# In-projection of a hybrid decoder step: how the recurrent states leave the core

## The chip, the cores and the metric

The kernel runs on one core of one Trainium2 chip. The metric is the device time of one execution in microseconds (us). The engines are TensorE (PE: matmuls, its weight loads are PEld), VectorE (DVE), ScalarE (ACT), GpSimd (POOL) and SyncE (SP). SP and ACT also issue most of the DMAs, each into a queue of its own, and both queues are served by the same 16 DMA engines. An engine executes its instructions in the order in which they are written, and waits on semaphores (wait_ge).

## The reference

One inference step of a hybrid layer for a prompt of 2048 tokens (with 16 meta tokens ahead of it, 2064 rows) and for 8 sample rows with a paged cache. The part that matters here is the recurrent branch and what it returns:

```python
def rg_lru_branch(xr, gr, conv_buf, h0, lp):
    xc, conv_new = causal_dwconv(xr, conv_buf, lp['rnn_conv_w'], lp['rnn_conv_b'])
    ...                                   # gates r and i from 8 blocks of 64x64, a = exp(log_a)
    u = jnp.sqrt(-jnp.expm1(2.0 * log_a)) * (i * xc.astype(jnp.float32))
    h = linear_recurrence(a, u, h0.astype(jnp.float32))
    y = h * jax.nn.gelu(gr.astype(jnp.float32))
    return y.astype(xr.dtype), h[:, -1], conv_new
```

h[:, -1] is 512 numbers for the prompt (output rnn_h_prompt) and 8 x 512 for the samples (rnn_h_sample). Everything is fp32.

## The kernel before

All activations are kept transposed: channels on the 128 partitions, the 2080 token columns (2064 prompt, 8 sample, 8 of padding) along the row, in 5 blocks of 416. The in-projection is a list of 21 chunks of 128 output channels. A chunk is 5 blocks, and a block is 24 matmuls of 128x416 (8 pieces of the inner dimension, each as three products of split fp32 halves, L2154). PE writes block j of a chunk into PSUM bank j, DVE copies it to ZS (L1603), ACT stores it to DRAM.

Chunks 0 to 8 give the inputs of the recurrent branch (xrT, grT in DRAM) and the forget logits. Chunks 9 to 20 are four groups c = 0 to 3 of three chunks (q, k, v of 128 channels), written as a hardware loop of two turns with two groups each (`with e.Fori(0, 2) as i` and `for u in range(2)`, c = 2i + u). Beside these matmuls each group also runs 128 channels of the recurrent branch, in this order:

- ACT waits until the group before has its result mixT stored (r_st, L1157), and loads RX from xrT (L1158). RX is both the input and, later, the result.
- DVE makes the causal convolution RC out of RX (L1680, three times L1683, and three small ones for the samples, the last is L1695). It does so in turn with the copies of the q chunk's five blocks: copy 0, step, copy 1, step, and so on.
- PE, after the first block of the k chunk, waits for all copies of q and turns the tail of q (L2218), then waits for the convolution and does the gate matmuls (L2225, L2226). After each of the other blocks of k there is another pair of gate matmuls.
- ACT makes the gates, the decay RA and the factor RW, DVE multiplies, scans (L1728 writes the states h over all columns into RW) and adds the samples' step (L1732, semaphore r_sc). Then DVE writes mixT's values into RX (L1737, r_y).
- ACT, in its handling of the v chunk: after block 2 it stores the states (L1207, L1209), after block 3 it stores RX to mixT (L1213).

The rows of k and v are outputs with tokens as rows. So PE turns each block with four transposes into PSUM bank 5 (turn_rows, L2211), ACT copies the bank to a buffer TS (take_rows, L1134 and L1135) and stores it as rows of 512 bytes (L1138, L1142). There are 11 such events a group; t_pe counts PE's side, t_ev ACT's copies, and the two slots of TS are released by t_st[0] and t_st[1], which count landed DMAs. PE turns block j-1 of a chunk after it has computed block j, and block 4 of v right after the turn of block 3, at the group's end (L2237).

The state stores of the kernel before take the last prompt column of RW, [128 partitions x 1], and the 8 sample columns, [128 x 8], and write each element to its place in DRAM, where the 128 channels lie side by side and the samples 2048 bytes apart: 128 + 1024 elements of 4 bytes a group. The semaphore r_ho counts them; ACT waits for it before it overwrites RW in the next group, and at the end of the phase.

After the loop, SP loads the first head's q and k (fetch_head(0), L545 to L550; it waits for the last matmul, the q and k stores and POOL's memsets), ACT waits for all stores and counts up phase_end, and the attention phase begins when these loads have landed (L1747, L1226) and all engines have counted phase_end.

Of the kernel before, what the change touches and what calls it, by code (L numbers as in the profile page):

```python
# [17 lines left out]
ACT = mybir.ActivationFunctionType  # L18
AX = mybir.AxisListType

P = 128
# [14 lines left out]
TPR = NMETA + SEQ  # L36
NS = 8
TP = 2080
# [168 lines left out]
def build(nc, a, out):  # L207
    ctx = ExitStack()
    with ctx:
# [3 lines left out]
        def sem(name):  # L213
            return ctx.enter_context(nc.semaphore(name))
# [19 lines left out]
        identF = sb("identF", [P, P], F32)  # L234
# [31 lines left out]
        TS = sb("TS", [P, 2, 4, P], F32, m1)  # L266
        RX = sb("RX", [P, TP + 3], F32, m1)
        RC = sb("RC", [P, TP], F32, m1)
        RW = sb("RW", [P, TP], F32, m1)
# [134 lines left out]
        t_pe = sem("t_pe")  # L404
# [9 lines left out]
        r_gw = sem("r_gw")  # L414
        r_gl = sem("r_gl")
        r_st = sem("r_st")
        r_ho = sem("r_ho")
        r_conv = sem("r_conv")
        r_gate = sem("r_gate")
        r_act = sem("r_act")  # L420
# [92 lines left out]
        @block.sync  # L513
        def _(e):

            for s in (*x_st, *t_st, *z_st, r_st, r_gate, r_act, r_ho, r_y, t_pe, t_ev, pv, kf, df, vd, mr, *ao_st, od_s,
                      at_s, *tt_st, tt_ev, *go_st, gcv, tt_pe, y_tp, y_tk):
                e.sem_inc(s, 1)

# [517 lines left out]
        def _(e):  # L1037
# [92 lines left out]
            def take_rows(ev, slot, stored, j, kv, c):  # L1130
# [12 lines left out]
                if j == NB - 1:  # L1143
                    e.dma_start(one_k[kv][:, f], TS[NMETA:NMETA + NS, slot, 3]).then_inc(t_st[slot], 16)

            with e.Fori(0, 2) as i:

                plan = []
                count = [0, 0]
                for v in range(22):  # L1150
                    m = v % 11
                    plan.append((v % 2, count[v % 2]))
                    count[v % 2] += 16 * (1 if m == 0 else 3 if m in (5, 10) else 2)
                for u in range(2):
                    c = 2 * i + u
                    n = 9 + 3 * c
                    e.wait_ge(r_st, 16 * c + 1)  # L1157
                    e.dma_start(RX[:, 3:3 + TP], xrT[bass.ds(c * P, P), :]).then_inc(r_ld, 16)  # L1158
                    e.wait_ge(r_gate, 5 * c + 1)
                    e.wait_ge(c_gw, 1)  # L1160
                    for g, w in enumerate((a["w_rg_a"], a["w_rg_x"])):
                        for b in range(2):
                            e.dma_start(gw[64 * b:64 * b + 64, g, 64 * b:64 * b + 64], w[0][2 * c + b])\
                                .then_inc(r_gw, 16)

                    def event(m):
                        slot, before = plan[11 * u + m]
                        return 4 + 22 * i + 11 * u + m, slot, (128 if slot == 0 else 0) + count[slot] * i + before

                    for j in range(NB):  # L1170
                        store_block(n, j, qT[bass.ds(c * P, P), :], z_st)
                    take_tail(*event(0))
                    slot = event(0)[1]
                    e.dma_start(qrow[:, bass.ds(c * P, P)], TS[NMETA:NMETA + NS, slot, 0]).then_inc(t_st[slot], 16)
                    for j in range(NB):
                        store_block(n + 1, j, kT[bass.ds(c * P, P), :], z_st)

                        e.wait_ge(r_gate, 5 * c + j + 2)
                        if j:
                            e.wait_ge(r_u, 5 * c + j)  # L1180
                        e.sem_inc(go, 1)
                        e.activation(RT[:, 0], PS[:, 7, 0:BW], ACT.Tanh, bias=hb[:, bass.ds(c, 1), 1], scale=0.5)\
                            .then_inc(r_act, 1)
                        e.activation(RT[:, 1], PS[:, 6, 0:BW], ACT.Tanh, bias=hb[:, bass.ds(c, 1), 0], scale=0.5)\
                            .then_inc(r_act, 1)
                        e.wait_ge(r_act, 22 * c + 4 * j + 3)
                        if j == 0:
                            e.wait_ge(r_ho, 32 * c + 1)
                            e.wait_ge(r_y, c + 1)
                        e.sem_inc(go, 1)  # L1190
                        e.activation(RW[:, cols(j)], RT[:, 1], ACT.Tanh, bias=sp[:, bass.ds(c, 1), 0],
                                     scale=sp[:, bass.ds(c, 1), 0]).then_inc(r_act, 1)
                        e.activation(RA[:, cols(j)], RT[:, 1], ACT.Exp, bias=sp[:, bass.ds(c, 1), 6],
                                     scale=sp[:, bass.ds(c, 1), 6]).then_inc(r_act, 1)
                        take_rows(*event(1 + j), j, 0, c)
                    e.wait_ge(r_u, 5 * c + 5)
                    e.dma_start(RC[:], grT[bass.ds(c * P, P), :]).then_inc(r_gl, 16)
                    e.wait_ge(r_act, 22 * c + 21)
                    e.activation(RW[:], RW[:], ACT.Sqrt, scale=0.25).then_inc(r_act, 1)
                    for j in range(NB):  # L1200
                        take_rows(*event(6 + j), j, 1, c)
                        if j == 1:
                            e.wait_ge(r_gl, 16 * c + 16)
                            e.activation(RC[:], RC[:], ACT.Gelu_apprx_tanh).then_inc(r_act, 1)
                        if j == 2:
                            e.wait_ge(r_sc, c + 1)
                            e.dma_start(out["rnn_h_prompt"][0].rearrange("o n -> n o")[bass.ds(c * P, P), :],  # L1207
                                        RW[:, TPR - 1:TPR]).then_inc(r_ho, 16)
                            e.dma_start(out["rnn_h_sample"][0].rearrange("s n -> n s")[bass.ds(c * P, P), :],  # L1209
                                        RW[:, TPR:TPR + NS], allow_slow_non_contiguous=True).then_inc(r_ho, 16)  # L1210
                        if j == 3:
                            e.wait_ge(r_y, c + 2)
                            e.dma_start(mixT[bass.ds(DATT + c * P, P), :], RX[:, 3:3 + TP]).then_inc(r_st, 16)  # L1213

            e.wait_ge(t_st[0], 865)
            e.wait_ge(t_st[1], 737)
            e.wait_ge(r_st, 65)
            e.wait_ge(r_ho, 129)
            for s in z_st:
                e.wait_ge(s, 257)  # L1220
            e.wait_ge(r_act, 22 * 4 + 1)
            e.wait_ge(t_ev, 49)
            e.sem_inc(phase_end, 1)
            e.wait_ge(c_att2, 2)
            e.wait_ge(st_ld, 80)
# [304 lines left out]
        def _(e):  # L1530
# [125 lines left out]
            with e.Fori(0, 2) as i:  # L1656
                g_steps.start(i, 2 * 13)
                for u in range(2):
                    c = 2 * i + u
                    n = 9 + 3 * c  # L1660
                    ev = 4 + 11 * c
                    one = bass.ds(c, 1)

                    def tap(k):
# [459 lines left out]
        def _(e):  # L2124
# [75 lines left out]
            with e.Fori(0, 2) as i:  # L2200
                for u in range(2):
                    c = 2 * i + u
                    n = 9 + 3 * c
                    ev = 4 + 11 * c

                    def turn_rows(done, ev, j):

                        e.wait_ge(g_ev, done)
                        e.wait_ge(t_ev, ev + 1)
                        for m, (o, w) in enumerate(seg(j)):  # L2210
                            mm = e.transpose(PS[0:w, 5, m * P:(m + 1) * P], ZS[:, j, o:o + w], identF[:])  # L2211
                        mm.then_inc(t_pe, 1)

                    def after_k(j):
                        if j == 0:
                            e.wait_ge(g_ev, 5 * n + 10)
                            e.wait_ge(t_ev, ev + 1)
                            e.transpose(PS[0:TAIL, 5, 0:P], ZS[:, NB - 1, 3 * P:BW], identF[:]).then_inc(t_pe, 1)  # L2218
                        else:
                            turn_rows(5 * (n + 1) + j - 1 + 6, ev + j, j - 1)  # L2220

                        e.wait_ge(r_conv, c + 1)
                        e.wait_ge(r_gw, 64 * c + 64)
                        e.wait_ge(r_act, 22 * c + (4 * j - 1 if j else 1))
                        e.matmul(PS[:, 6, 0:BW], gw[:, 0], RC[:, cols(j)], start=True, stop=True)  # L2225
                        e.matmul(PS[:, 7, 0:BW], gw[:, 1], RC[:, cols(j)], start=True, stop=True).then_inc(r_gate, 1)  # L2226

                    def after_v(j):
                        if j == 0:
                            turn_rows(5 * (n + 1) + 4 + 6, ev + 5, NB - 1)  # L2230
                        else:
                            turn_rows(5 * (n + 2) + j - 1 + 6, ev + 5 + j, j - 1)

                    chunk(n, (1 + u) % 2)
                    chunk(n + 1, u % 2, after_k)
                    chunk(n + 2, (1 + u) % 2, after_v)
                    turn_rows(5 * (n + 2) + 4 + 6, ev + 10, NB - 1)  # L2237
            e.wait_ge(g_mm, 5 * NIN)
            e.wait_ge(t_pe, 49)
            e.wait_ge(r_gate, 21)  # L2240
            e.sem_inc(phase_end, 1)

# [372 lines left out]
```

## Time and profile before

| | |
|---|---|
| device time, 3 runs | 3356.98, 3363.10, 3363.46 us, median 3363.1 |
| the profiled execution | 3355.78 us, its span 3353.6 us |
| TensorE busy | 91% of the span |
| granted TensorE clock | 0.942 of full speed, mean |
| the four groups of the in-projection | about 335 to 694 us of the span |
| first matmul of the attention phase | 724.96 us |

The profile's times are counted from the start of the span. A query of the trace can be cut to a window of it. The granted clock is given as a share of full speed; 1.00 is the 2.4 GHz level, 0.50 the 1.2 GHz level.

### The profile page before, as it was taken

Reading aid. Unit: us, or ns where it says so; the run is one execution under the profiler, and the core shown is the slowest. Engines: PE = TensorE matmul, PEld = TensorE weight load, DVE = VectorE, ACT = ScalarE, POOL = GpSimd, SP = SyncE. Lnnn points to the kernel's source line nnn. Section 1 sums busy time; section 2 is a strip of 40 time slices with the busy share of each in tenths; the row PEclk is TensorE's granted clock in tenths of the full one; section 3 lists DMA queues with packets and bytes.
Section 4 is the critical chain, followed back from the end, with each engine's and each line's share of the span. In section 5 each row is a group of like instructions: output and inputs, shape, how many; then the busy total and the mean of one; then the engine's idle time right before and its main releaser. Section 6 shows DMA issues by size and latency. Waiting matters only on the chain.

```text
span 3353.6 us, 46822 instructions
## 1 busy us (share of the span) xinstructions
PE 3037.8 (91%) x15400; PEld 2659.0 (79%) x15400; DVE 1447.2 (43%) x1910; ACT 757.9 (23%) x1529; POOL 1212.9 (36%) x575
## 2 busy tenths in 40 slices
PE   4798998957788888897899999999999998999998
PEld 4798987843354545455898999999999998999998
DVE  4212433348566555534415445555445554222221
ACT  5100332212232333333202000000000002434343
POOL 1011111133566565633766222222222222455443
PEclk7899999967799898998899999999999999999999
DMA  5211343355787677754345111111111114555553
GB/s 182 94 65 55 90 104 94 86 106 160 237 250 231 182 228 236 229 174 136 113 132 154 44 47 51 51 42 48 45 42 51 51 38 155 183 182 188 180 194 110
DMA packets 253580, 422.52 MB, mean 126 GB/s; under 512 B 49265, under 2 KB 156954, under 8 KB 248906
## 3 DMA queue, kind: packets, MB, share of 16 engines
q1 hardware_dynamic: 167986, 322.58, 30.8%
q10 hardware_dynamic: 85152, 97.07, 9.6%
q8 instruction: 68, 1.11, 0.1%
q0 software_dynamic: 288, 1.05, 0.1%
q14 instruction: 86, 0.70, 0.1%
HBM read 337.21 MB, written 83.46 MB: 125 GB/s over the span
## 4 chain that ended last, share of the span: by engine, by line
PE 69%; DMA 7%; POOL 7%; DVE 6%; issue 5%; SPq 4%; ACT 2%; ACTq 0%; POOLq 0%; DVEq 0%
PE PS L2452 33%; PE PS L2154 13%; PE PS L2534 4%; PE PS L2536 4%; PE PS L2535 4%; POOL prod L905 3%; DMA Kpg<-in_cache_k 2%; PE PS L2346 2%; SPq L581 2%; PE PS L2443 1%; SPq L574 1%; DMA xin<-in_x_prompt 1%; PE PS L2135 1%; DVE YT L2097 1%; DMA mixT<-RX 1%
## 5 line engine op out<-in xcount | busy, mean ns | idle before, releaser
L2452 PE MATMUL PS<-MH,VS 128*128 128x416 f32 x4000 | 1086.9, 352 | 11.2 <-POOL VS L968 9.0
L2452 PEld LDWEIGHTS PS<-MH,VS 128*128 128x128 f32 x4000 | 750.1, 188 | 23.2 <-issue 12.3
L2452 PE MATMUL PS<-ML,VS 128*128 128x416 f32 x2000 | 701.4, 351 | 0.0
L962 POOL TENSOR_TENSOR VR<-VR,gains 128x1024 f32<-128x1024 f32 x52 | 98.7, 1898 | 791.6 <-PE PS L2452 694.9
L2452 PEld LDWEIGHTS PS<-ML,VS 128*128 128x128 f32 x2000 | 376.7, 188 | 4.2 <-issue 0.8
L1025 POOL TENSOR_TENSOR DL<-DR,DH 128x1408 fp32r<-128x1408 f32 x80 | 258.6, 3233 | 286.1 <-ACT DH L1446 286.0
L905 POOL TENSOR_TENSOR prod<-Kpg,qb 128x1024 f32<-128x1024 f32 x118 | 284.0, 2407 | 174.0 <-DMA Kpg<-in_cache_k 137.9
L2346 PE MATMUL PS<-PT,VA 128*65 128x416 f32 (+16 forms) x816 | 340.0, 501 | 4.0 <-ACT PT L1307 3.5
L2534 PE MATMUL PS<-GH,DH 128*128 128x416 f32 x880 | 314.3, 357 | 16.2 <-DVE GL L2079 8.6
L2154 PE MATMUL PS<-XH,WH 128*128 128x416 f32 x840 | 307.2, 366 | 19.8 <-issue 11.6
L2536 PE MATMUL PS<-GH,DL 128*128 128x416 f32 x880 | 310.5, 353 | 0.0
L2535 PE MATMUL PS<-GL,DH 128*128 128x416 f32 x880 | 308.4, 350 | 0.0
L2255 PE MATMUL PS<-KA,QA 68*128 68x512 f32 (+3 forms) x360 | 222.1, 639 | 90.1 <-DVE MP L1757 55.8
L1307 ACT ACTIVATE PT<-PS 128x416 f32<-128x416 f32 (+16 forms) x408 | 186.5, 459 | 501.1 <-PE PS L2332 335.6
L2154 PE MATMUL PS<-XH,WL 128*128 128x416 f32 x840 | 297.1, 354 | 0.0
L2154 PE MATMUL PS<-XL,WH 128*128 128x416 f32 x840 | 296.5, 353 | 0.0
L1419 ACT ACTIVATE GC<-GC 128x416 f32<-128x416 f32 x110 | 60.8, 553 | 824.6 <-DVE GC L2032 746.1
L1757 DVE TENSOR_REDUCE MP<-PS 128x1 f32<-128x512 f32 (+3 forms) x360 | 206.2, 600 | 83.6 <-PE PS L2255 49.8
L2062 DVE TENSOR_TENSOR GP<-PS,R 128x416 f32<-128x416 f32 x110 | 64.9, 592 | 364.9 <-PE PS L2452 364.6
L2255 PEld LDWEIGHTS PS<-KA,QA 68*128 68x128 f32 (+1 forms) x360 | 73.8, 206 | 179.6 <-DVE MP L1757 105.0
L1806 DVE TENSOR_REDUCE scw<-prod 128x16 f32<-128x1024 f32 x128 | 155.4, 1214 | 102.2 <-POOL prod L905 101.5
L841 POOL CAST WH<-WR 128x1024 fp32r<-128x1024 f32 x21 | 24.3, 1158 | 461.1 <-PE PS L2154 454.2
(273 smaller groups left out, 4501.7 us busy)
## 6 DMA issues: line engine op xcount, KB each, us to landing
Kpg<-in_cache_k SPq DMA_DIRECT2D x256, 256.0 KB, 4.2
Vpg<-in_cache_v SPq DMA_DIRECT2D x256, 256.0 KB, 4.1
DR<-in_w_down SPq DMA_DIRECT2D x80, 704.0 KB, 4.1
gT<-GO ACTq DMA_DIRECT2D x110, 208.0 KB, 1.9
VR<-in_w_up SPq DMA_DIRECT2D x44, 512.0 KB, 3.5
GRb<-gT SPq DMA_DIRECT2D x31, 416.0 KB, 5.1
WR<-in_w_stream SPq DMA_DIRECT2D x21, 512.0 KB, 3.6
GRa<-gT SPq DMA_DIRECT2D x24, 416.0 KB, 5.8
```

What stands on the lines that cost most here:

```text
L905: e.tensor_tensor(prod[:, g % 4], Kpg[:, g % 4], qb[:, v].unsqueeze(1).to_broadcast([P, 2, DATT]), ALU.mult).then_inc(kpp, 1)
L1025: e.tensor_tensor(DL[h][:], DR[:, h], DH[h][:].bitcast(F32), ALU.subtract).then_inc(d_lo, 1)
L1307: e.activation(PT[0:kr, t % 3, 0:n], PS[0:kr, (u + t) % 2, 0:n], ACT.Exp, scale=0.125).then_inc(ex, 1)
L1757: e.tensor_reduce(MP[0:rows, qt, pc:pc + 1], PS[0:rows, banks[p % len(banks)], 0:n], AX.X, ALU.max).then_inc(mx, 1)
L1806: e.tensor_reduce(sc[:, v, 2 * g:2 * g + 2, :], p.rearrange("p b (h d) -> p b h d", d=HD), AX.X, ALU.add)\
L2154: mm = e.matmul(PS[:, j, 0:BW], w[:, u, k], x[:, k, cols(j)], start=(k == 0 and q == 0), stop=(k == KC - 1 and q == 2))
L2255: mm = e.matmul(o[:, 0:n], QA[0:HD + 4, v, qt * P:qt * P + rows], KA[0:HD + 4, v, k0:k0 + n], start=True, stop=not diag)
L2346: e.matmul(PS[0:HD + 1, 4 + (u + j) % 2, o:o + n], VA[0:kr, u, kt], PT[0:kr, t % 3, 0:n], start=(kt == 0), stop=t in ENDS).then_inc(pv, 1)
L2452: mm = e.matmul(PS[:, j, 0:BW], w[:, u, k], x[:, k, cols(j)], start=(k == 0 and q == 0), stop=(k == KC - 1 and q == 2))
L2534: e.matmul(PS[:, v, 0:BW], DH[h][:, k], GH[:, r, m], start=(kk == 0), stop=False)
L2535: e.matmul(PS[:, v, 0:BW], DH[h][:, k], GL[:, r, m], start=False, stop=False)
L2536: e.matmul(PS[:, v, 0:BW], DL[h][:, k], GH[:, r, m], start=False, stop=(kk == FC - 1))\
```

## The change

The last prompt state and the sample states are now the columns TPR-1 to TP-1 of RW, 17 in all (8 of them padding). PE turns them with one transpose into 17 rows of 128 in PSUM bank 5, as a twelfth event of the group; ACT copies them to a slot of TS and stores row 0 to rnn_h_prompt and rows 1 to 8 to rnn_h_sample, each row 512 bytes. The element stores and the semaphore r_ho go. The counts of events per group go from 11 to 12.

```diff
+            def take_states(ev, slot, stored, c):
+                e.wait_ge(t_pe, ev + 2)
+                e.wait_ge(t_st[slot], stored + 1)
+                e.activation(TS[0:TP - TPR + 1, slot, 0], PS[0:TP - TPR + 1, 5, 0:P], ACT.Copy).then_inc(t_ev, 1)
+                e.wait_ge(t_ev, ev + 2)
+                f = bass.ds(c * P, P)
+                e.dma_start(out["rnn_h_prompt"][0][:, f], TS[0:1, slot, 0]).then_inc(t_st[slot], 16)
+                e.dma_start(out["rnn_h_sample"][0][:, f], TS[1:1 + NS, slot, 0]).then_inc(t_st[slot], 16)
...
                         if j == 0:
-                            e.wait_ge(r_ho, 32 * c + 1)
                             e.wait_ge(r_y, c + 1)
...
-                        if j == 2:
-                            e.wait_ge(r_sc, c + 1)
-                            e.dma_start(out["rnn_h_prompt"][0].rearrange("o n -> n o")[bass.ds(c * P, P), :],
-                                        RW[:, TPR - 1:TPR]).then_inc(r_ho, 16)
-                            e.dma_start(out["rnn_h_sample"][0].rearrange("s n -> n s")[bass.ds(c * P, P), :],
-                                        RW[:, TPR:TPR + NS], allow_slow_non_contiguous=True).then_inc(r_ho, 16)
                         if j == 3:
                             e.wait_ge(r_y, c + 2)
                             e.dma_start(mixT[bass.ds(DATT + c * P, P), :], RX[:, 3:3 + TP]).then_inc(r_st, 16)
+                    take_states(*event(11), c)
...
                     turn_rows(5 * (n + 2) + 4 + 6, ev + 10, NB - 1)
+                    e.wait_ge(r_sc, c + 1)
+                    e.wait_ge(t_ev, ev + 12)
+                    e.sem_inc(go, 1)
+                    e.transpose(PS[0:TP - TPR + 1, 5, 0:P], RW[:, TPR - 1:TP], identF[:]).then_inc(t_pe, 1)
```

PE's wait on t_ev means: ACT has copied the eleventh event (the last block of v) out of bank 5. In DVE's program only the count changes (ev = 4 + 12c): its waits on t_pe for the q chunk's blocks now name one event later than before, all of them issued by PE ahead of the block that DVE copies.

## Rows read from the trace of the kernel before

**Rows 1.** Waits of PE, 335 to 700 us: us in total, times, longest.

```profile
PE PS L2218 <- DVE ZS L1603: 13.0, 2, 7.3
PE PS L2154 <- issue: 11.6, 1, 11.6
...
PE PS L2225 <- DVE RC L1695: 1.8, 2, 0.9
```

**Rows 2.** The chain of waits, 396 to 530 us: start, us, what.

```profile
417.30 14.45 DMA mixT<-RX
...
431.91 5.54 DMA RX<-xrT
...
452.53 1.75 PE PS L2225 x2
454.28 1.39 PE PS L2226 x2
455.66 5.51 PE PS L2154 x24
...
461.62 0.70 PE PS L2225 x2
...
463.01 4.54 PE PS L2154 x24
```

**Rows 3.** DMA issues: queue, count, KB each, median us from issue to landing.

```profile
xT<-xst ACTq DMA_DIRECT2D x16, 512.0 KB, 3.8
...
RX<-xrT ACTq DMA_DIRECT2D x4, 1040.0 KB, 5.1
...
mixT<-RX ACTq DMA_DIRECT2D x4, 1040.0 KB, 14.2
```

**Rows 4.** Tile RW, the sample states' store: ns min/median/max, first and last start.

```profile
L1209 ACTq DMA_DIRECT2D out_rnn_h_sample<-RW x4: 394/396/403, 412.7 to 690.4; - x4
```

**Rows 5.** Timeline of ACT, 504.6 to 505.2 us: the same store in the second group.

```profile
504.81 0.40 ACTq L1209 DMA_DIRECT2D out_rnn_h_sample<-RW  x1
```

**Rows 6.** Stretches: length, busy PE, PEld, DVE, ACT, POOL; clock, DMA share, GB/s.

```profile
462.00:482.00 20.00, 20.00 (x100) 17.29 (x99) 5.06 (x9) 9.70 (x20) 1.44 (x2) 1.00 0.20 65
508.00:512.90 4.90, 0.66 (x4) 0.37 (x4) 0.00 (x0) 0.21 (x2) 2.57 (x2) 0.94 0.83 51
...
417.30:428.60 11.30, 11.30 (x62) 11.17 (x61) 0.59 (x1) 0.64 (x2) 1.31 (x1) 1.00 1.10 48
428.60:431.70 3.10, 3.10 (x18) 3.06 (x17) 0.00 (x0) 0.00 (x0) 0.00 (x0) 1.00 0.87 293
...
694.60:706.70 12.10, 0.00 (x0) 0.00 (x0) 0.00 (x0) 0.64 (x2) 3.02 (x1) 0.58 1.11 48
706.70:720.70 14.00, 0.00 (x0) 0.00 (x0) 0.00 (x0) 0.00 (x0) 0.00 (x0) 0.50 0.87 215
```

**Rows 7.** The chain of waits, 618 to 650 us.

```profile
641.68 4.74 PE PS L2154 x24
```

**Rows 8.** Lines L2200 and L2407, PE's loops: their branches, ns min/median/max.

```profile
L2200 PEldq COMPARE_BRANCH  x2: 79/5979/11879, 508.4 to 693.6; - x2
...
L2407 PEldq COMPARE_BRANCH  x3: 76/223/4338, 1102.0 to 1471.0; - x3
```

**Rows 9.** The chain, 690 to 770 us, and from the waits of SP.

```profile
700.07 20.61 DMA Kst<-kT
...
SPq L625 <- ACTq L1223: 17.7, 1, 17.7
```

**Rows 10.** Timeline 413 to 422.5 us: last turn of a group, ACT's copy of it.

```profile
416.09 0.66 PE L2211 MATMUL PS<-identF,ZS 128*128 128x128 f32 x4 [0.73 <-ACT TS L1135]
...
418.22 0.25 ACT L1135 ACTIVATE TS<-PS 32x128 f32<-32x128 f32 x1
```

**Rows 11.** A stretch in which PE idles, columns as in rows 6.

```profile
2821.90:2824.70 2.80, 0.00 (x0) 0.00 (x0) 2.80 (x2) 1.77 (x2) 1.89 (x1) 1.00 0.78 299
```

**Rows 12.** Line L1142, ACT's issues of the v rows: ns min/median/max.

```profile
L1142 ACTq DMA_DIRECT2D out_v_prompt<-TS x20: 446/520/3968, 402.2 to 696.3; - x20
```

More of the change, by code:

```diff
@@ L416, in build @@
         r_st = sem("r_st")
-        r_ho = sem("r_ho")
         r_conv = sem("r_conv")
@@ L514, in _ @@
         def _(e):
-            for s in (*x_st, *t_st, *z_st, r_st, r_gate, r_act, r_ho, r_y, t_pe, t_ev, pv, kf, df, vd, mr, *ao_st, od_s,
+            for s in (*x_st, *t_st, *z_st, r_st, r_gate, r_act, r_y, t_pe, t_ev, pv, kf, df, vd, mr, *ao_st, od_s,
                       at_s, *tt_st, tt_ev, *go_st, gcv, tt_pe, y_tp, y_tk):
@@ L1149, in _ @@
                 count = [0, 0]
-                for v in range(22):
-                    m = v % 11
+                for v in range(24):
+                    m = v % 12
                     plan.append((v % 2, count[v % 2]))
@@ L1166, in event @@
                     def event(m):
-                        slot, before = plan[11 * u + m]
-                        return 4 + 22 * i + 11 * u + m, slot, (128 if slot == 0 else 0) + count[slot] * i + before
+                        slot, before = plan[12 * u + m]
+                        return 4 + 24 * i + 12 * u + m, slot, (128 if slot == 0 else 0) + count[slot] * i + before
                     for j in range(NB):
@@ L1213, in _ @@
                             e.dma_start(mixT[bass.ds(DATT + c * P, P), :], RX[:, 3:3 + TP]).then_inc(r_st, 16)
-            e.wait_ge(t_st[0], 865)
-            e.wait_ge(t_st[1], 737)
+                    take_states(*event(11), c)
+            e.wait_ge(t_st[0], 128 + 2 * count[0] + 1)
+            e.wait_ge(t_st[1], 2 * count[1] + 1)
             e.wait_ge(r_st, 65)
-            e.wait_ge(r_ho, 129)
             for s in z_st:
@@ L1221, in _ @@
             e.wait_ge(r_act, 22 * 4 + 1)
-            e.wait_ge(t_ev, 49)
+            e.wait_ge(t_ev, 53)
             e.sem_inc(phase_end, 1)
@@ L1660, in _ @@
                     n = 9 + 3 * c
-                    ev = 4 + 11 * c
+                    ev = 4 + 12 * c
                     one = bass.ds(c, 1)
@@ L2203, in _ @@
                     n = 9 + 3 * c
-                    ev = 4 + 11 * c
+                    ev = 4 + 12 * c
                     def turn_rows(done, ev, j):
@@ L2237, in _ @@
                     turn_rows(5 * (n + 2) + 4 + 6, ev + 10, NB - 1)
+                    e.wait_ge(r_sc, c + 1)
+                    e.wait_ge(t_ev, ev + 12)
+                    e.sem_inc(go, 1)
+                    e.transpose(PS[0:TP - TPR + 1, 5, 0:P], RW[:, TPR - 1:TP], identF[:]).then_inc(t_pe, 1)
             e.wait_ge(g_mm, 5 * NIN)
-            e.wait_ge(t_pe, 49)
+            e.wait_ge(t_pe, 53)
             e.wait_ge(r_gate, 21)
```

## The prediction

> **What bounds the kernel now.** TensorE is busy for 91% of the span (the table above), so what counts in the in-projection is where PE stands still. I read the waits first. PE's waits over the four groups (335 to 700 us) are few [rows 1]: two at L2218 for DVE's copies, 13.0 us together (7.3 the longer, so 5.7 the other), the two for the convolution right behind them (1.8 us), and one of 11.6 us for which the profile shows no releaser.
>
> The chain of waits, read next, says what stands behind the first of them [rows 2]. The store of mixT out of RX, issued at 417.30, takes 14.45 us; only then can RX be loaded again (5.54 us, to 437.45); only then does DVE convolve, in turn with its copies of q's blocks, and PE gets to its gate matmuls at 452.53. The fourth group is the same picture.
>
> Why does that store take 14 us? The list of DMAs has it at a median of 14.2 us for 1040 KB, the load of the same 1040 KB at 5.1, and a store of 512 KB at 3.8 [rows 3]. The stretches show when the DMA engines are slow [rows 6]: from 417.3 to 428.6 they are fully busy (share 1.10, packets overlap) and move 48 GB/s; from 428.6 to 431.7 they move 293 GB/s. The one thing in that queue that is unlike the rest is the pair of state stores, 1152 elements of 4 bytes, the second of them issued at 412.7 [rows 4]. The slow time ends 16 us after it (412.7 to 428.6), and again in the last group (690.4 to 706.7). In the second group the engines are already slow from 508 to 512.9 (share 0.83, 51 GB/s), 3 us after the states' store at 504.8 [rows 5], and before mixT's store is issued. The k rows, stored in rows of 512 bytes as the v rows are, leave the engines at a share of 0.20 for 65 GB/s (462 to 482). So neither mixT nor the rows are the cause: the elements are, and each set of them clogs both DMA queues for about 16 us.
>
> Beside this: the Trainium skill's page "DMA: Bandwidth & Descriptors", section "Specifications", says that a transfer below 512 bytes is done as read-modify-write, which agrees in kind. But the same page, section "Why small descriptors are slow (HBM only)", gives only some 3 cycles of overhead a packet; by that rule the 1152 packets are 72 on each of 16 engines, 4 cycles each, some 0.3 us at the page's 850 MHz (an estimate from that page), and there would be nothing to win. The measured stretches speak against it; it is kept as rival 2.
>
> **The change part by part.** The elements go, and with them the clog. It costs now, in four places:
>
> (a) Second group. PE idles 7.3 + 0.9 us and comes back with the clock at half: the gates take 1.75 + 1.39 against the next pair's 463.01 - 461.62 = 1.39, the first block 5.51 against 4.54 [rows 2]. Together 8.2 + 1.75 + 0.97 = 10.9 us. Afterwards: mixT's store lands after 5.1 us (the load of that size) to 7.7 (the 512 KB store scaled). I take 6, so RX lands at 417.3 + 6 + 5.5 = 428.8 in place of 437.5. From its landing to the first gates DVE needs 452.5 - 437.5 = 15.1 us, so it is ready at 444, by the upper end at 445.6. PE, with the new wait counted, is not there before q's five blocks and k's first, 6 x 4.54 = 27.2 us after 418.9: 446. The whole stall goes.
>
> (b) Fourth group: 5.7 + 0.9 us idle, the gates 1.75 over as in (a), the block 4.74, 0.2 over [rows 1, 7]: 8.6 us. It goes for the same reason.
>
> (c) The 11.6 us without a releaser, ahead of the third group. It is the loop's own branch: PE's branch at L2200 takes 11.88 us on its taken turn, at 508.4, in the middle of the clog; the other far branch, L2407, takes 4.34 at most [rows 8]. I take it that code is loaded through the same engines, and that 4.3 us remain: 7.5 us gained, bounds 0 (this branch is slow by itself) and 11.7 (as short as 0.2, the median of L2407). The Trainium skill's page "Runtime: NRT & Kernel Launch", section "Instruction fetch mechanics", says that a taken branch out of the fetched window makes a DMA of the target, which execution waits for; the row agrees, and by that rule other DMAs can delay it. What is late next in the third group: RX, which lands sooner too, since ACT's issue of v rows no longer takes 3.97 us there in place of 0.52 [rows 12]. I expect no stall.
>
> (d) The end of the phase. The last load of the first head is issued at 700.07 and lands at 720.7 [rows 9]. The engines move 48 GB/s for 12.1 us, then 215 for 14.0 [rows 6]: 581 + 3010 KB, 3.6 MB. At 215 to 293 GB/s these bytes need 12.3 to 16.7 us, from about 696, so they land at 708.4 to 712.8. I take 710.7: 10 us sooner, bounds 8 and 12. SP's wait for ACT's phase_end [rows 9] is for row stores in the same clog and moves along; the state rows stored last are 4.5 KB.
>
> What it adds: at each group's end PE waits for ACT's copy of the last turn. The turn ends at 416.75, the copy at 418.47 [rows 10], because ACT still issues v rows and mixT before it: 1.7 us, and some 0.5 for the semaphore and one transpose (four take 0.66). That is 2.2 us, three times on the path, 6.6 us; behind it stand the next q blocks, or the branch, and for them DVE's copies. The fourth costs nothing, as SP's loads wait for POOL's memsets. Lower bound 0.5 a time (the copy comes at once); upper bound 2.2 + 2.7 with the clock loss of (a). An idle stretch of 2.8 us leaves the clock at 1.00 [rows 11], so I take no clock loss. ACT gets one more small copy (0.25 us, rows 10), and its two issues (0.4 us each, rows 4) move from after v's block 2 to behind the last v rows, at about 421; there it would wait for mixT's landing at 423 anyway. They are no longer ahead of mixT. The wait on r_sc was met two blocks before, the r_ho waits are met as long as the clog is over, and DVE's later counts of t_pe are met by PE's order: nothing for these.
>
> Sum: 10.9 + 8.6 + 7.5 + 10 - 6.6 = 30.4 us. The profiled execution took 3355.8 us, so 3325 by it. It is 7.3 us under the median of the runs; the four executions together have a mean of 3359.8, and from that I go to 3330. After the phase nothing waits for a fixed time, so the gain is carried on.
>
> **Rivals.**
> 1. A part stays: the branch keeps its 11.9 us (for it: L2407 jumps over other code and is no measure of L2200; against it: the branch ends with the clog), and the clock drops once in the new gaps or the end gains only 8. 30.4 - 7.5 - 2.5 = 20 us, 3340.
> 2. The other side: elements are cheap, and the slow stretch belongs to v rows and mixT together. Then every stall stays, and PE's new wait comes on top. In the second and fourth group it is absorbed, as RX sets the stall there. Ahead of the third, ACT's copy is late by the slow issue, 1.7 + 3.97 - 0.52 = 5.2 us [rows 10, 12], and the branch starts after it; at the end the state rows, last in the queue, delay phase_end by some 2 us. 3359.8 + 7 = 3367. It decides if the engines still move about 50 GB/s behind mixT's issue. Against it: 508 to 512.9 is slow before that issue, and k rows clog nothing [rows 6].
> 3. More than the sum: the branch is hidden (11.7), the end gains 12, the new waits are 1.7: 10.9 + 8.6 + 11.7 + 12 - 5.1 = 38 us, 3322.
>
> **How the numbers follow.** Forecast 0.65, rival 1 0.20, rival 3 0.07, rival 2 0.05, and 0.03 for a gain undone later without a loss. The range, 3318 to 3346, goes from rival 3 with a fast set of runs to rival 1 with a slow one. About 0.2%, 6.7 us, is what can be told from no change. Slower is 0.04 (rival 2 ends just at the bound, so 0.01 of it is no change), the same 0.05 (with the undone gain and 0.01 of rival 1), faster 0.91.
>
> **What would show it.** mixT's store at 5 to 8 us in the list of DMAs, and some 250 GB/s behind its issue; no wait at L2218; PE's branch at L2200 at about 4 us; the last load of the first head landing some 10 us after its issue; a wait of PE of about 2 us for ACT's copy at each group's end. The forecast is wrong if mixT's store stays at 14 us, or if PE's new wait grows because ACT's copy waits for a slot of TS.

## The result, and the profile after

| | before | after |
|---|---|---|
| device time, median (lowest to highest) | 3363.3 us (3357.0 to 3367.2, 4 runs) | 3337.1 us (3329.2 to 3339.5, 4 runs) |
| ratio, 95% interval | | 0.9912, 0.9887 to 0.9938 |
| profiled execution, its span | 3355.8, 3353.6 us | 3329.2, 3327.0 us |

The change saves 26 us; 33 were forecast from the medians (3363 to 3330), 30.4 from the profile. The time, 3337, lies within the range of 3318 to 3346. The two profiled executions differ by 26.6 us, so they can be compared part by part. In the profile after, the lines of the code have moved by a few: L2154 is now L2156, L2211 is L2213, L2225 and L2226 are L2227 and L2228, L1135 is L1134. The new turn of the states is L2243.

The waits of PE over the groups (335 to 690 us), to be read against [rows 1]:

```profile
PE PS L2243 <- ACT TS L1134: 7.8, 4, 2.1
PE PS L2156 <- issue: 5.9, 1, 5.9
PE PS L2213 <- ACT TS L1134: 3.2, 4, 0.8
```

Both waits for DVE's copies are gone, and so are those for the convolution; the wait without a releaser is down from 11.6 to 5.9 us. The new wait for ACT stands there four times, 2.1 us the longest. The store of mixT, from the list of DMAs:

```profile
mixT<-RX ACTq DMA_DIRECT2D x4, 1040.0 KB, 4.2
```

It was 14.2 [rows 3]. The chain of waits from 396 to 530 us, where the store of mixT and the load of RX stood [rows 2]:

```profile
417.87 0.27 PE PS L2243
418.15 29.00 PE PS L2156 x144
447.27 0.90 PE PS L2227 x2
448.17 0.70 PE PS L2228 x2
448.86 4.53 PE PS L2156 x24
...
503.17 5.88 issue
509.05 20.96 PE PS L2156 x98
```

No DMA is in it any more; PE goes through q and the first block of k (144 matmuls) without a break. But these take 29.00 us, where six blocks at 4.54 us are 27.2. The stretches tell why (columns as in [rows 6]: the third number from the end is the granted clock, the last one GB/s). The first two begin with the issue of mixT's store, in the first and in the second group; the other three follow on each other at the first group's end:

```profile
416.60:420.80 4.20, 2.91 (x9) 2.62 (x10) 0.00 (x0) 0.90 (x3) 0.92 (x1) 0.71 0.89 296
...
501.60:505.80 4.20, 0.27 (x1) 0.09 (x1) 0.00 (x0) 0.91 (x3) 1.23 (x1) 0.75 0.89 307
414.90:418.30 3.40, 1.07 (x6) 0.62 (x7) 0.00 (x0) 0.81 (x4) 2.54 (x2) 1.00 0.50 180
418.30:421.70 3.40, 3.40 (x11) 3.22 (x12) 0.00 (x0) 0.27 (x1) 0.00 (x0) 0.50 0.99 305
421.70:425.10 3.40, 3.40 (x19) 3.35 (x18) 0.54 (x1) 0.00 (x0) 0.00 (x0) 0.99 1.02 338
```

Behind mixT's issue the engines move 296 GB/s in place of 48. And the clock is at the half level (0.50, 1.2 GHz) from 418.3 to 421.7, after a stretch in which PE was busy for 1.07 us of 3.4. The fourth group is the same picture (28.97 us for its six blocks). PE's loop branch, and the loading of the first head at the phase's end:

```profile
L2202 PEldq COMPARE_BRANCH  x2: 79/2899/5719, 503.0 to 679.8; - x2
```

The branch takes 5.72 us on its taken turn; it took 11.88 [rows 8]. The last load of the first head is issued at 683.74, and ACT's first work on it (L1228) starts at 694.3, 10.5 us later, where it landed after 20.6 [rows 9].

Where the time came from, by the end of each group's last turn of v and the first matmul of the attention phase:

| stretch | before | after | gain | forecast |
|---|---|---|---|---|
| up to the end of the first group | 416.75 | 415.79 | 1.0 | 0 |
| second group | 92.2 | 85.3 | 6.9 | 10.9 - 2.2 = 8.7 |
| third group | 95.4 | 91.5 | 3.9 | 7.5 - 2.2 = 5.3 |
| fourth group | 89.8 | 85.3 | 4.5 | 8.6 - 2.2 = 6.4 |
| to the first matmul of attention | 30.8 | 20.5 | 10.3 | 10 |
| the rest | 2628.6 | 2628.6 | 0 | 0 |

The 1.0 us of the first line is no gain of the change: the first group ends at 415.79 here and at 417.78 in a second trace of the same kernel.

### The profile page after: what moved, and what is told of

It reads as the page before. It is cut to its first block, busy times and chain, and to the rows that moved or that the text cites. A ratio compares the mean times of both kernels' runs of the same rounds, so it can differ in the third digit from the quotient of the medians.

```text
span 3327.0 us, 46844 instructions
## 1 busy us (share of the span) xinstructions
PE 3034.3 (91%) x15404; PEld 2655.5 (80%) x15404; DVE 1449.8 (44%) x1910; ACT 759.5 (23%) x1533; POOL 1212.0 (36%) x575
## 3 DMA queue, kind: packets, MB, share of 16 engines
q1 hardware_dynamic: 167986, 322.58, 30.8%
## 4 chain that ended last, share of the span: by engine, by line
PE 73%; POOL 7%; DMA 6%; DVE 5%; issue 4%; SPq 4%; ACT 1%; ACTq 0%; POOLq 0%; DVEq 0%
PE PS L2458 33%; PE PS L2156 15%; PE PS L2540 4%; PE PS L2542 4%; PE PS L2541 4%; PE PS L2352 3%; POOL prod L904 3%; DMA Kpg<-in_cache_k 2%; SPq L580 2%; PE PS L2449 1%; SPq L573 1%; DMA xin<-in_x_prompt 1%; PE PS L2137 1%; PE PS L2336 1%; DVE MP L1759 1%
## 5 line engine op out<-in xcount | busy, mean ns | idle before, releaser
L2156 PE MATMUL PS<-XH,WH 128*128 128x416 f32 x840 | 307.0, 365 | 14.1 <-DVEq L1601 7.1
L2156 PE MATMUL PS<-XH,WL 128*128 128x416 f32 x840 | 297.4, 354 | 0.0
L2156 PE MATMUL PS<-XL,WH 128*128 128x416 f32 x840 | 297.0, 354 | 0.0
```

The costliest lines, as they stand in the source:

```text
L2156: mm = e.matmul(PS[:, j, 0:BW], w[:, u, k], x[:, k, cols(j)], start=(k == 0 and q == 0), stop=(k == KC - 1 and q == 2))
```

## The experiments

All of the runs that have an interval were timed beside the kernel before (3363.9 us median) on one chip. The others have a profile and one time, beside 3361.2 and 3359.8 us.

### The change once more

Its edit is the diff above.

> The change itself once more, beside the others on the same chip. 0.9912 of the kernel before was measured; the sum of its parts in the two traces is 26.5 us, so a ratio of 0.992. If the gain were an accident of one set of runs, the ratio would be above 0.995.

Measured: 3336.8 us (3322.9 to 3348.0), ratio 0.9911, interval 0.9890 to 0.9932. The gain is the same in a second set of runs. The profile repeats the first: waits of 2.08, 1.80 and 2.08 us at L2243, 5.74 at the branch.

### The states left out

```diff
-                        if j == 2:
-                            e.wait_ge(r_sc, c + 1)
-                            e.dma_start(out["rnn_h_prompt"][0].rearrange("o n -> n o")[bass.ds(c * P, P), :],
-                                        RW[:, TPR - 1:TPR]).then_inc(r_ho, 16)
-                            e.dma_start(out["rnn_h_sample"][0].rearrange("s n -> n s")[bass.ds(c * P, P), :],
-                                        RW[:, TPR:TPR + NS], allow_slow_non_contiguous=True).then_inc(r_ho, 16)
...
```

This is the kernel before without its state stores; the semaphore r_ho and the waits on it go too. The states are not output.

> The kernel before without both state stores; the states are not output at all. Theory: the 4-byte stores alone clog the DMA queues, so this has the whole gain of the change and none of its new waits. Each new wait of PE costs 2.1 us of idling, 0.3 of transposing and about 1.7 for one 3.4 us stretch at half clock, three times on the path: 12 us. So 26 + 12 = 38 us under the kernel before, ratio 0.989, mixT's store at 4.2 us, no wait at L2218, no clock loss at the starts of the second and fourth group. Rival (the clock falls at the group ends anyway, because of the 0.8 us wait there): 26 + 7 = 33 us. Rival (part of the clog is due to mixT beside the v rows): mixT's store stays above 7 us.

Measured: 3320.2 us (3314.3 to 3323.3), ratio 0.9876, interval 0.9855 to 0.9897: 43.6 us under the kernel before, 16.6 under the change. Waits of PE, 335 to 700 us:

```profile
PE PS L2246 <- DVE KA L1739: 20.9, 1, 20.9
PE PS L2145 <- issue: 3.8, 1, 3.8
PE PS L2202 <- ACT TS L1134: 3.1, 4, 0.8
```

Those of q's copies and of the convolution are gone, without any other change to the code: the elements alone made them. (The 20.9 us are the wait for the first matmul of attention, which the window of the change's list above left out.) mixT's store takes 4.5 us, and on SP's queue, where the longest load of weights took 16.0 us in the kernel before, the longest now takes 6.0: the elements had slowed both queues. The last three groups take 81.2, 86.5 and 81.1 us, 13.3 less together than in the change: the price of the three new waits (the theory said 12). The clock stays full at the starts of the second and fourth group, though the short wait for ACT (0.73 us at both) is still there. In the first of these stretches PE waits, at 412.4; the others are behind it (columns as before):

```profile
411.40:414.80 3.40, 2.67 (x18) 2.32 (x17) 0.59 (x1) 0.64 (x2) 2.61 (x2) 1.00 0.21 61
413.00:416.40 3.40, 3.30 (x19) 3.25 (x20) 0.00 (x0) 0.68 (x3) 2.55 (x2) 1.00 0.54 200
416.40:419.80 3.40, 3.40 (x20) 3.36 (x19) 0.59 (x1) 0.00 (x0) 0.00 (x0) 1.00 0.98 320
```

The six blocks behind it take 27.20 and 27.19 us. So the small wait alone does not lower the clock, and that rival falls. By the medians the whole is larger than the 38 us of the theory. By the profiles it is 41.4 us: 3.0 before the first group is done, 28.6 in the three groups, 9.9 from there to the first matmul of attention. The 3.0 can't be put down to the stores: over the six traces of the kernels before, after and of these experiments the first group ends anywhere from 413.8 to 418.4 us.

### The turn of the states in the middle of v's last block

```diff
+                    def turn_states(j):
+                        if j == NB - 1:
+                            e.wait_ge(r_sc, c + 1)
+                            e.wait_ge(t_ev, ev + 10)
+                            e.sem_inc(go, 1)
+                            e.transpose(PS[0:TP - TPR + 1, 5, 0:P], RW[:, TPR - 1:TP], identF[:]).then_inc(t_pe, 1)
...
-                    chunk(n + 2, (1 + u) % 2, after_v)
-                    turn_rows(5 * (n + 2) + 4 + 6, ev + 10, NB - 1)
-                    ...
+                    chunk(n + 2, (1 + u) % 2, after_v, turn_states)
+                    turn_rows(5 * (n + 2) + 4 + 6, ev + 11, NB - 1)
```

turn_states is called after 12 of a block's 24 matmuls, and does something in the last block only. ACT takes and stores the states after v's block 2, ahead of mixT.

> The change, with the states turned in the middle of v's last block instead of after the group's last turn: r_sc and ACT's copy of the turn before are both done by then, so PE should wait for nothing. Theory: 2.1 us of idling and the clock loss go at three group ends, 11 us under the change, 37 under the kernel before. If the clock falls at these ends because of the 0.8 us wait for ACT alone, only 6 us under the change. Rival on the other side: the turn stands in the middle of an accumulation, and breaks the stream of weight loads; then each costs up to the 0.3 us of the turn itself and ACT's copies of v blocks come later: 5 us under the change at most.

Measured: 3324.8 us (3321.6 to 3334.6), ratio 0.9892, interval 0.9872 to 0.9912; 39 us under the kernel before, 12 under the change (the intervals of the two ratios overlap a little). The three groups take 81.3, 87.9 and 81.2 us, 11.7 less than the change's, as the theory had it. From the timeline of PE, 411 to 419 us:

```profile
413.65 0.27 PE L2244 MATMUL PS<-identF,RW 128*17 128x128 f32 x1
416.05 0.60 PE L2216 MATMUL PS<-identF,ZS 128*128 128x128 f32 x4
417.74 0.66 PE L2216 MATMUL PS<-identF,ZS 128*128 128x128 f32 x4 [1.09 <-ACT TS L1134]
```

The states' turn has no idle time before it, and the next group starts right after the last turn, which itself waits 1.09 us in place of 0.81. The six blocks of the second and fourth group take 27.19 and 27.18 us, so the clock loss is gone with the wait. The branch is shorter too, at line L2205:

```profile
L2205 PEldq COMPARE_BRANCH  x2: 79/1819/3559, 499.1 to 668.2; - x2
```

3.56 us against 5.72. In the change it starts at 503.0, 1.4 us after the issue of mixT's store (307 GB/s from 501.6 to 505.8, above); here it starts at 499.1, 1.1 us before that issue. By the profiles this kernel is only 7.6 us under the change; in its trace the first group ends 2.6 us later.

### The same without PE's loop

```diff
-            with e.Fori(0, 2) as i:
+            for i in range(2):
```

Only in PE's program; the instructions of the four groups are then written out one after the other.

> As the last, and PE's loop over the four groups written out, so that PE has no branch ahead of the third group (the other engines keep their loops). Theory: the 5.7 us of the branch are the loading of code at a jump; straight code is fetched ahead, so another 5.7 us and 1.7 of clock go: 7 us under the last, ratio 0.987 of the kernel before. Rival: ACT's own branch (9.6 us before) then holds the third group, because RX is loaded behind it; PE would wait at L2218 for some us and the gain is 2 us or less. Rival: PE's code is longer and some other place pays for its loading; then nothing is gained.

Measured: 3320.9 us (3317.8 to 3323.3), ratio 0.9877, interval 0.9857 to 0.9898. The waits of PE:

```profile
PE PS L2267 <- DVE KA L1751: 20.9, 1, 20.9
PE PS L2216 <- ACT TS L1134: 4.2, 4, 1.2
...
PE PS L2230 <- DVE RC L1698: 1.4, 1, 1.4
```

The wait without a releaser is gone: it was the jump. The third group takes 83.0 us in place of 87.9, so 4.9 are gained of the 7 expected. With the loop it lost 3.3 us of idling at the branch and 3.0 in the six blocks behind it (30.17 us against 27.2, at a lowered clock). Both are gone, but the first rival is there in small: PE now waits 1.4 us for the convolution, whose RX is loaded behind ACT's own branch (at 501.2; the load is issued at 505.5). In the medians it is 4 us under the kernel with the loop, which the intervals don't separate. This is the fastest kernel that gives all outputs: 43 us under the kernel before.

### Which elements clog the queues

Seven kernels of before with one state store a group (r_ho counts it); all but the first leave the prompt's store out. The edits, one kernel or, for d bytes (64, 32, 16), one kind a line:

```
 prompt only:       the samples' store left out (128 elements of 4 bytes, side by side)
 samples only:      the prompt's store left out (1024 elements, 8 rows of 128 side by side)
 samples, 512 apart: e.dma_start(apart[bass.ds(c * P, P), :, 0], RW[:, TPR:TPR + NS], ...)        # apart (512, 8, 128)
 samples, 32 bytes: e.dma_start(beside[bass.ds(c * P, P), :], RW[:, TPR:TPR + NS])                # beside (512, 8)
 samples, d apart:  e.dma_start(apart[:, bass.ds(c * P, P), 0].rearrange("s n -> n s"), RW[...])  # apart (8, 512, d/4)
```

> The kernel before without the samples' store: 128 elements of 4 bytes a group stay, which lie side by side in 512 bytes of DRAM; the samples' states are not output. If the clog goes with the number of elements (16 us for 1152, 14 ns each), it lasts 2 us and mixT's store takes 4 to 6 us. If it is the collision of 128 partitions in the same 512 bytes, this store alone has a good part of it: mixT above 8 us.

> The kernel before without the prompt's store: 1024 elements of 4 bytes a group stay; the prompt's states are not output. By the number of elements the clog lasts 14 us and mixT's store takes 12 us. If the prompt's store was the cause, mixT is at 5 us.

> As the last, but the 1024 elements are written 512 bytes apart into a scratch tensor, no two of them in the same 512 bytes (the states are not output). If an element costs what it costs by itself (read, modify, write), the clog is as long as with the real layout: mixT's store 12 us. If the cost comes from neighbours in one line that wait for each other, it is gone: 4 to 6 us.

> As the last but one, with the 8 states of a channel written side by side: 128 packets of 32 bytes a group into a scratch tensor, the same 4 KB (the states are not output). By the number of packets: 2 us of clog, mixT 4 to 6 us. If small bytes in shared lines are what costs, whatever the number, mixT stays well above that.

> The 1024 elements of the samples' states in the real order (sample by sample, channels side by side), but each 64 bytes from the next, in a scratch tensor; the states are not output. Side by side (4 bytes) they clogged the queues, mixT's store at 15.6 us; 512 bytes apart they did not, 4.1 us. Theory: what costs is that writes of several partitions meet in one small unit of DRAM. If the unit is 64 bytes or less, mixT is at 4 to 5 us here; if it is 512 bytes, 8 elements still meet and mixT stays above 6 us.

> The same 32 bytes apart: clear (4 to 5 us) if the unit is 32 bytes, partly clogged if it is 64 (two elements meet: 5 to 8 us).

> The same 16 bytes apart, so that four elements meet in 64 bytes and two in 32. If every meeting costs the same, the clog is a quarter or an eighth of the 16 us (2 to 4 us, mixT 4 to 6 us); if it is all or nothing, mixT is above 10 us.

Measured, for one store a group:

| store | elements or packets | mixT's store, min/median/max us | one time, us |
|---|---|---|---|
| both (the kernel before) | 1152 of 4 bytes, side by side | 13.9/14.2/16.3 | 3355.8 |
| samples | 1024 of 4 bytes, side by side | 13.6/15.6/18.8 | 3355.5 |
| prompt | 128 of 4 bytes, side by side | 6.9/8.2/10.8 | 3327.6 |
| samples, 16 bytes apart | 1024 of 4 bytes | 4.4/7.0/9.0 | 3315.5 |
| samples, 32 bytes apart | 1024 of 4 bytes | 4.0/4.1/5.7 | 3328.9 |
| samples, 64 bytes apart | 1024 of 4 bytes | 4.0/4.1/5.7 | 3324.6 |
| samples, 512 bytes apart | 1024 of 4 bytes | 4.0/4.1/9.5 | 3326.2 |
| samples, 32 bytes side by side | 128 of 32 bytes | 4.0/4.1/6.6 | 3316.9 |
| none | | 4.0/4.5/5.6 | 3320.2 (median) |

The stretches behind mixT's issue, first with the samples alone, whose store was issued at 411.6, then with the prompt alone, issued at 410.6:

```profile
417.20:427.50 10.30, 10.30 (x56) 10.19 (x55) 0.59 (x1) 0.64 (x2) 0.83 (x1) 1.00 1.02 45
427.50:430.00 2.50, 2.50 (x15) 2.47 (x14) 0.00 (x0) 0.00 (x0) 0.00 (x0) 1.00 0.86 309
```

```profile
416.20:420.80 4.60, 4.60 (x26) 4.54 (x25) 0.59 (x1) 0.64 (x2) 0.84 (x1) 1.00 0.94 92
420.80:423.00 2.20, 2.20 (x14) 2.18 (x13) 0.00 (x0) 0.00 (x0) 0.00 (x0) 1.00 0.96 357
```

It is not the number of elements: 1024 of them 32 bytes apart or more leave mixT's store at 4.1 us, and 128 side by side, an eighth of the samples' number, clog the engines for 10 us (410.6 to 420.8) against 16 (411.6 to 427.5). It is not their size either, for those that leave the store alone are of 4 bytes too. What matters is how near to each other separate writes fall: 4 bytes (15.6 us), 16 bytes (7.0 us, still slow), 32 bytes and more (4.1, clear). A unit of 32 bytes fits this, with eight elements in it side by side, two when 16 bytes apart and one when 32 bytes apart; that it is a unit, and not only a distance, no run tests. The 7.0 us lie between the two outcomes that were expected for 16 bytes (4 to 6, or above 10).

The stores themselves landed in 7.3 us (prompt), and in 7.9, 4.0, 2.7 and 3.1 us (samples 16, 32, 64 and 512 bytes apart), against 1.4 us for the 128 packets of 32 bytes. So 32 bytes apart is not yet quite as cheap as 64.

My theory that each element costs 14 ns fell here: it gave the 128 elements 2 us of clog, and mixT's store behind the samples 512 bytes apart 12 us; 10 and 4.1 were measured. The kernel with packets of 32 bytes does not decide, as both theories let it be clear. Whether the slow part is the DRAM or the DMA engines waiting for each other's writes can't be seen in these profiles; what is shown is the distance.

PE's branch goes with the clog. In all of these kernels it starts 1.0 to 1.1 us before mixT's issue, and takes 11.60 us with the samples side by side, 5.42 with the prompt alone, 4.74 with 16 bytes, and 3.62 to 4.24 in the others.

The single times are no measure of these differences: they vary by more than 10 us between kernels whose mixT store is alike.

## Why the prediction was right

**The cause.** The elements clog both queues: shown by leaving them out (mixT's store on ACT's queue 14.2 to 4.5 us, the longest load of weights on SP's 16.0 to 6.0). The second rival, that v rows and mixT were slow by themselves, is refuted by the same run and by the change (296 GB/s behind mixT's issue). The reading of the stretches, slow before mixT was issued and for 16 us after each state store, was enough to tell this beforehand. What the reading left open is why. The prediction names the 1152 elements and no more, and what counts is how near they lie to each other. For this change it makes no difference, since in rows of 512 bytes no two separate writes lie that near. The Trainium skill's page "DMA: Bandwidth & Descriptors" gives, in "Specifications", a limit of 512 bytes, below which a transfer is a read-modify-write. The runs agree that small writes can be slow, and show that size alone does not make the clog: 4-byte writes 32 bytes apart leave the store behind them at 4.1 us.

**(a) and (b), the two stalls.** Right: no wait at L2218's place, and the convolution in time. mixT's store took 4.2 us, under the 5.1 that I had as the lower bound from the load; nothing hung on it, as PE was the later one.

**(c), the branch.** Right in kind: the kernel without the loop shows that the idling was the jump, and the kernels with other state stores that it is longer in the clog. It was put at 4.3 us and took 5.7. The new wait is in this too, as it moves the branch behind mixT's issue: where the clog is gone and the branch starts before that issue, it takes 3.56 to 4.24 us (six kernels), and behind it 5.72 and 5.58 (the two traces of the change).

**(d), the end.** 10 forecast, 10.3 measured, and carried whole: the 2628.6 us behind it are the same in both profiles.

**The new waits.** This is the term that was mis-sized: 2.2 us each without a clock loss, 6.6 together. The idle time was right (2.08, 1.80, 2.08 us and 0.27 for the turn), and so was ACT's copy as its end. The clock was not: "an idle stretch of 2.8 us leaves the clock at 1.00 [rows 11], so I take no clock loss." At the group's end PE also waits 0.8 us for ACT and turns two blocks in little pieces, so it was busy for 1.07 us of the 3.4 before the clock fell, while around [rows 11] it was at work without a break. The six blocks behind it took 29.0 us in place of 27.2: 1.8 us in the second and in the fourth group. Without the 2.1 us wait they take 27.2 (the states left out, and the turn in mid-block), so the loss comes with that wait; why 2.8 us of idling elsewhere cost nothing is not shown. That and the branch's 1.4 are the 5 us by which the groups fell short of the forecast (15.3 against 20.4); without the state rows and their waits the three groups gained 28.6. The profiles differ by 26.6 us and not by 25.6 only because the first group happened to end 1.0 us sooner.

## What to carry to other kernels

A store that is slow for its size is slow for what stands ahead of it: look for the last odd DMA before the slow time begins, in any queue, and see whether the time that the engines stay slow is tied to its issue. Single elements that lie side by side in DRAM and come from different partitions are such a DMA; turn them into rows, or at least write them 32 bytes apart, better 64. A turn on PE that needs another engine's copy belongs in the middle of a block, where the copy is long done; at the group's end it cost the wait here, and the clock behind it.

## What the runs showed of the hardware

- Separate 4-byte writes side by side in DRAM, one partition each, slow the core's DMAs down for 10 us (128 of them in one row of 512 bytes) to 16 us (1024 in eight rows). Behind mixT's issue the engines then moved 92 and 45 GB/s on average, in place of about 300; the longest load of weights in the other queue took 16.0 us with both stores, and 6.0 without them. At 16 bytes apart the store behind them takes 7.0 us, at 32, 64 or 512 bytes apart 4.1, and 4.5 with no such writes at all.
- PE's jump back over a loop whose turn lasts some 170 us takes 3.56 to 4.24 us where it starts 1 us before the issue of a 1040 KB store and nothing clogs the engines, 5.6 to 5.7 where it starts some 1.4 us after that issue, and 11.9 in the clog.
- The granted clock fell to the half level (1.2 GHz) at a group's end with small transposes between a wait of 0.8 us and one of 2.1 us, though PE had waited 2.8 us elsewhere [rows 11] without it. With the 0.8 us wait alone it stayed at 2.4 GHz.
